# Late modulation products in a streaming encoder step: from the projection units into the rounds of the recurrence

## The reference

```python
def layer(x, c, attn_fn, wkv0, shift0, w_ada, b_ada, g_norm, w_in, ...):
    mod = jax.nn.silu(c) @ w_ada + b_ada                  # (1024) @ (1024, 6144), for two c
    sh1, sc1, gt1, sh2, sc2, gt2 = jnp.split(mod[:, None, :], 6, axis=-1)
    h = rmsnorm(x, g_norm[0]) * (1 + sc1) + sh1
    z = h @ w_in                                          # 5376 columns
    ...                                                   # band attention; token shift
    o_b, wkv1 = rwkv7_time_mix(zx, wkv0, ...)             # delta-rule recurrence, 8 heads
    merged = gates[..., :D_MODEL] * (o_a @ w_out_attn) + gates[..., D_MODEL:] * (o_b @ w_out_rwkv)
    x = x + gt1 * (merged @ w_out)
    h2 = rmsnorm(x, g_norm[1]) * (1 + sc2) + sh2
    u, gg = jnp.split(h2 @ w_ffn_in, 2, axis=-1)
    x = x + gt2 * ((jax.nn.silu(gg) * u) @ w_ffn_out)
```

## Time and profile before

| | |
|---|---|
| median of three runs | 1021.21 us (1020.38 to 1023.74) |
| the profiled execution | 1022.72 us, its span in the trace 1021.0 us |
| busy share of the span | PE 96%, PEld 88%, DVE 66%, ACT 49%, POOL 34% |
| projection by seven products | 68 to 194 us of the span |
| rounds of the recurrence | 312.7 to 496 us, with the tail to about 520 us |
| granted PE clock | 0.996 of full |

### The profile page before, as it was taken

The page is one execution under the profiler, slowest core; times in us unless marked ns, Lnnn a source line. Parts: engine busy times, 40 slices in busy tenths (PEclk is TensorE's granted clock), DMA queues, the critical chain, the costliest instruction groups (busy, mean ns, idle before and its releaser), DMA issues.

```text
span 1021.0 us, 26935 instructions
## 1 busy us (share of the span) xinstructions
PE 978.5 (96%) x10820; PEld 893.8 (88%) x10820; DVE 670.6 (66%) x1420; ACT 496.3 (49%) x1118; POOL 344.7 (34%) x341
## 2 busy tenths in 40 slices
PE   6999999999999999898899999999999999999996
PEld 4898888999997677666798999999999999999996
DVE  4985565595036666666547566888888887966724
ACT  4565655463444454545242255555555555723423
POOL 1156432153313260600260455343343343043340
PEclk9999999999999999999999999999999999999998
DMA  9967676483301000020342632223323323222312
GB/s 355 393 180 258 208 250 232 157 273 117 119 35 50 14 13 24 13 87 4 129 124 73 215 102 82 83 82 100 106 82 97 109 82 98 87 83 78 115 37 88
DMA packets 107372, 123.50 MB, mean 121 GB/s; under 512 B 5300, under 2 KB 91488, under 8 KB 104840
## 3 DMA queue, kind: packets, MB, share of 16 engines
q1 hardware_dynamic: 102048, 112.97, 34.0%
q10 hardware_dynamic: 5224, 9.10, 2.8%
HBM read 109.45 MB, written 15.23 MB: 122 GB/s over the span
## 4 chain that ended last, share of the span: by engine, by line
PE 85%; DVE 7%; ACT 4%; issue 2%; POOL 1%; ACTq 1%; DVEq 0%
PE ps L2460 45%; PE ps L3132 22%; PE ps L2658 11%; PE ps L3198 4%; PE ps L2873 1%; DVE s_sb L1925 1%; PE ps L2773 1%; DVE hl L1616 1%; DVE Pb L1896 1%; ACT x_sq L977 0%; POOL w_lo L765 0%; DVE XX L1906 0%; PE ps L3217 0%; POOL w_lo L930 0%; ACTq L963 0%
## 5 line engine op out<-in xcount | busy, mean ns | idle before, releaser
L924 POOL TENSOR_TENSOR ws_lo<-w_raw,ws_hi 128x512 fp32r<-128x512 f32 x63 | 80.5, 1292 | 146.2 <-DVE ps L2179 132.5
L765 POOL TENSOR_TENSOR w_lo<-w_raw,w_hi 128x2048 fp32r<-128x2048 f32 x11 | 50.7, 4608 | 140.6 <-ACT w_hi L987 123.8
L3132 PE MATMUL ps<-th,ws_hi 128*128 128x274 f32 x336 | 97.6, 291 | 0.0
L3132 PE MATMUL ps<-tl,ws_hi 128*128 128x274 f32 x336 | 97.6, 290 | 0.0
L3132 PE MATMUL ps<-th,ws_lo 128*128 128x274 f32 x336 | 97.2, 289 | 0.0
L2460 PE MATMUL ps<-hh,w_hi 128*128 128x274 f32 x448 | 95.7, 298 | 1.4 <-DVE hl L1616 0.7
L2460 PE MATMUL ps<-hl,w_hi 128*128 128x274 f32 x448 | 92.9, 291 | 2.4 <-DVE al L2261 2.1
L2460 PE MATMUL ps<-hh,w_lo 128*128 128x274 f32 x448 | 93.4, 292 | 0.0
L2460 PEld LDWEIGHTS ps<-hh,w_hi 128*128 128x128 f32 x448 | 71.7, 191 | 7.2 <-issue 5.8
L2186 DVE TENSOR_TENSOR ws_lo<-ps,ws_hi 128x512 fp32r<-128x512 f32 x84 | 57.3, 684 | 28.8 <-ACT ws_hi L1384 28.8
L3132 PE MATMUL ps<-hh,ws_hi 128*128 128x274 f32 x252 | 74.8, 297 | 0.6 <-ACT rest L1409 0.3
(11 more groups left out here) (549 smaller groups left out, 3031.4 us busy)
## 6 DMA issues: line engine op xcount, KB each, us to landing
w_raw<-in_w_ffn_in SPq DMA_DIRECT2D x44, 512.0 KB, 4.9
w_raw<-in_w_in SPq DMA_DIRECT2D x42, 512.0 KB, 5.8
ada_l<-in_w_ada SPq DMA_DIRECT2D x16, 1024.0 KB, 5.0
ada_w<-in_w_ada SPq DMA_DIRECT2D x8, 1024.0 KB, 13.4
w_raw<-in_w_ffn_out SPq DMA_DIRECT2D x16, 512.0 KB, 3.5
g_d<-gst SPq DMA_DIRECT2D x16, 274.0 KB, 2.6
gring<-g_d SPq DMA_DIRECT2D x16, 274.0 KB, 3.7
w_raw<-in_w_out SPq DMA_DIRECT2D x8, 512.0 KB, 4.6
```

What stands on the lines that cost most here:

```text
L765: pool.tensor_tensor(w_lo[:, s, 0:cols], w_raw[:, s, 0:cols], w_hi[:, s, 0:cols].bitcast(F32), ALU.subtract).then_inc(lo_done, 1)
L924: pool.tensor_tensor(slot_of(ws_lo, p), block_source(s, p), slot_of(ws_hi, p).bitcast(F32), ALU.subtract) .then_inc(wslo_done, 1)
L3132: ins = pe.matmul(product_out(s, p), wt[:, w], xt[c], start=fresh and c == 0 and j == 0, stop=c == HK - 1 and j == 2, skip_group_check=not ...
```

## The change

- The 16 late blocks leave `proj_seven`, with their two copies, flips and bias adds.
- They come back as 32 pieces. Piece m belongs to row block k = m // 4 and column quarter b = m % 4, and takes both sections: two sections by four strips of 32 partitions, 128 columns each, 8 matmuls in the code, 16 in the trace. Sections share the bank by a shift of the stationary window (`c_columns`), so that section 1 lands in rows 0 and 1 and section 2 in rows 2 and 3 of each strip.
- Pieces run in phases 4, 7, 8 and 10 of every round, behind the level products of the phase and ahead of its `p_attn`. A piece uses bank 3, which the recurrence leaves free in these phases.
- A row block is complete after one round. DVE adds the bank to a sum in SBUF (`late_add`, at phase 10, ahead of that phase's attention work on DVE); PE waits for it at phase 12. One flip (`late_flip`) and the bias adds go into the tail's first two levels.
- SP issues the loads of piece m when piece m - 2 is done: for even m two transfers of 256 KB, for odd m four (two of 192 KB and two of 64 KB). All rows are 512 bytes. The first two are issued ahead of the first K and V slices, and the first half of w_out_attn moves behind the loads of piece 29.

```diff
+        LATE_P = [16 * r + p for r in range(NR_) for p in (4, 7, 8, 10)]
...
+            def late(m):
+                (k, b), q = late_at(m), m % 2
+                if m >= 2:
+                    sp.wait_ge(late_used, m - 1)
+                for i in range(2):
+                    w = ada_rows(1 + i, k).rearrange("p (j b c) -> p j b c", j=4, c=P)[:, :, b, :]
+                    if q == 0:
+                        sp.dma_start(late_w[i][:, :, :], w).then_inc(late_in[0], 16)
+                    else:
+                        sp.dma_start(late_w[2 + i][:, :, :], w[:, 0:3]).then_inc(late_in[1], 16)
+                        sp.dma_start(late_last[i][:, :], w[:, 3]).then_inc(late_in[1], 16)
...
             for hp in range(HP):
+                asked = late_until(32 * hp - 15, asked)
                 if hp:
                     sp.wait_ge(kct_mm, hp)
                 sp.dma_start(kc_raw[:, :, :], ...)
+                asked = late_until(32 * hp - 2, asked)
...
+            def late_add(k):          # DVE
+                got, out = ps[:, LATE_BANK, :], late_sum[:, :, :].rearrange("p b c -> p (b c)")
+                dve.wait_ge(late_used, 4 * k + 4)
+                if k:
+                    dve.wait_ge(late_added, ADDED + k)
+                    tt(out, got, out, ALU.add).then_inc(late_added, 1)
+                else:
+                    dve.wait_ge(rg_out, RG_OUT + 16 * HP)
+                    dve.tensor_copy(out, got).then_inc(late_added, 1)
...
+                if p == 10:
+                    late_add(rnd)
                 v_attn(g)
...
+            def late_piece(m):        # PE
+                (k, b), q = late_at(m), m % 2
+                pe.wait_ge(late_in[q], 16 + (32, 64)[q] * (m // 2 + 1))
+                if b == 0 and k:
+                    pe.wait_ge(late_added, ADDED + k)
+                for i in range(2):
+                    for j in range(4):
+                        w = late_w[2 * q + i][:, j, :] if q == 0 or j < 3 else late_last[i][:, :]
+                        ins = pe.matmul(ps[32 * j:32 * j + 32, LATE_BANK, b * P:(b + 1) * P], c_columns(k, 1 + i), w,
+                                        start=i == 0, stop=i == 1)
+                ins.then_inc(late_used, 1)
...
-                    g = 7 * (i - U_PS) + p
-                    if g % 4 == 3 and g // 4 < NLATE:
-                        late(g // 4)
...
+                for m, u in enumerate(LATE_P):
+                    if u == g:
+                        late_piece(m)
                 if g:
                     p_attn(g)
```

More of the change, by code:

```diff
@@ L99, in build @@
         par = at("par", [P, N1 + N2], PERS + 1536)
[L100 to L103, removed]
+        sc2 = at("sc2", [P, KD * 32 + 8], PERS + 2080)
+        mod = at("mod", [P, 6 * KD, 2], PERS + 3136)
+        gsc = at("gsc", [P, 2, KD, 2], PERS + 3520)
+        stat = at("stat", [P, 16], PERS + 3648)
         shc = stat[:, 0:4].rearrange("p (n s) -> p n s", n=2)
[L105 to L107 removed]
+        omka = at("omka", [P, HP], PERS + 3520)
+        shst = at("shst", [P, 2, ZT], E + 76512)
+        ind = at("ind", [P, HP, 32], E + 73792)
         shrow = at("shrow", [2 * ZT, P], PERS + 512)
@@ L138, in build @@
         ada_w = [at(f"ada_w{k}", [P, UC], a) for k, a in enumerate(ADDR_EARLY)]
-        ada_l = [at(f"ada_l{q}", [P, UC], a) for q, a in enumerate(ADDR_LATE)]
+        late_w = [at("late_w0", [P, 4, P], HI + 4608), at("late_w1", [P, 4, P], RAW),
+                  at("late_w2", [P, 3, P], HI + 6656), at("late_w3", [P, 3, P], RAW + 6656)]
+        late_last = [at("late_l2", [P, P], RAW + 2048), at("late_l3", [P, P], PERS + 512)]
+        late_sum = at("late_sum", [P, 4, P], E + 74304)
         HK, QB = KD // 2, KD // 2 * P
@@ L407, in nth, with c_columns, late_at @@
             return base + per * (i - U_PS) + n
-        NLATE = (NSEC - 1) * KD
-        NFLIP = NSEC + 1
+        NLATE, NEARLY = KD * 4, 2
+        LATE_BANK, FLIP_BANK = 3, 5
+        def c_columns(k, sec):
+            return sc2[:, 32 * k + (0, 2, 0)[sec]:32 * k + (0, 2, 0)[sec] + 32]
+        def late_at(m):
+            return m // 4, m % 4
         T_QKV = 1
@@ L646, in _, with late_until @@
             sp.wait_ge(lo_done, U_OA)
+            late_free = [LATE_P[m - 2] for m in range(2, NLATE)]
+            def late_until(u, m):
+                while m < NLATE and late_free[m - 2] <= u:
+                    late(m)
+                    m += 1
+                return m
+            sp.wait_ge(shift_out, 32)
+            sp.wait_ge(unit_mm, U_OA)
+            sp.wait_ge(rg_out, RG_OUT + 16 * HP)
+            for m in range(2):
+                late(m)
+            asked = 2
             for hp in range(HP):
+                asked = late_until(32 * hp - 15, asked)
                 if hp:
@@ L1572, in _ @@
             p1 = lambda c: par[:, c:c + 1]
-            link(dve.memset(sc2[:, :, :], 0.0))
+            link(dve.memset(sc2[:, :], 0.0))
             dve.memset(ssq[TS:2 * TS, TT:KS], float(D))
@@ L2036, in _ @@
                     attn_part(0)
+                if lev == 1:
+                    dve.wait_ge(ada_tr, NEARLY + 1)
+                    mod_added(1)
+                    mod_added(2).then_inc(mod_set, 1)
+                    dve.wait_ge(mod_set, NEARLY + 1)
+                    scales(1)
             chain(7)
@@ L2499, in rstd_spread, with late_flip @@
                 ins.then_inc(xd_mm, 1)
[L2501 to L2510, removed]
+            def late_piece(m):
[9 more added lines that the diff above has]
+                ins.then_inc(late_used, 1)
+            def late_flip():
+                pe.wait_ge(late_added, ADDED + KD)
                 for b in range(4):
-                    ins = pe.transpose(ps[:, ACC, b * P:(b + 1) * P], ada_sb[:, b * P:(b + 1) * P], ident[:, :])
+                    ins = pe.transpose(ps[:, FLIP_BANK, b * P:(b + 1) * P], late_sum[:, b, :], ident[:, :])
                 ins.then_inc(ada_tr, 1)
@@ L2989, in _ @@
                 p_level_x(NT, lev)
+                if lev == 0:
+                    late_flip()
                 if lev < 3:
```

60 lines of the change are left out of this document (16 added, 44 removed).

## The result

The changed kernel takes 1027.62 us (median of 5 runs, 1025.16 to 1028.32), the kernel before 1021.21: ratio 1.0053, 95% interval 1.0035 to 1.0071. It is slower by 6.4 us, where I forecast 0.9 faster, and it lies outside my range. The profiled execution has a span of 1026.6 us against 1021.0, so 5.6 more.

A forecast was written before the change was run, and what follows sets the result against it. PE was taken as the bound, busy all 124.00 us of the projection and 188.40 of 208.00 in the recurrence. Terms -19.8 + 13.1 + 5.2 + 0.6 = -0.9 gave 1020.3 us from 1021.21, range 1017.5 to 1023.5.

The forecast's parts named there:

- What goes, -19.8: Projection: removing sixteen late blocks and two flips takes 19.8 us off PE's path.
- The rival in which the projection gives nothing back: Projection: block products newly wait for their weights, 0.5 us a unit, +5, so 1025; chance 0.09.
- A piece, 0.57: Recurrence: each piece costs PE 0.45 us plus 0.12 for one more change of form.
- the rival of weight loads in series: Pieces: weight loads not loaded ahead stand in series with matmuls, 32 x 0.43 = +13.8, so 1034; chance 0.14.
- The rounds, 4 x (1.40 + 1.88) = 13.1: Recurrence: pieces add 1.40 us to each even round and 1.88 to each odd one, over four pairs.
- the term of 0.68 for `late_add`: Odd rounds, phase 10: DVE works without pause, so the inserted add lengthens the round by 0.68 us; even rounds hide it.
- The stand for the fourth piece, 1.3 in each even round: Even rounds, phase 10: PE waits 1.3 us for piece 3's loads, issued only after piece 1; 5.2 us in four rounds.
- In the other places there is time: Recurrence: all loads other than the even rounds' fourth piece land before PE needs them, so no wait is counted.
- I count no change of it: Both stretches: granted clock stays 1.00, the 2.4 GHz level, as PE is never idle for long; no cost.
- The tail, 0.6: Tail: one flip costs PE 4 x 0.11 + 0.12 = 0.6 us; the bias adds cost nothing.
- The rival of the long stand: Even rounds' fourth piece: loads take 4.1 us to land, +5.6, so 1026; chance 0.06.
- The rival of loads in time: Even rounds' fourth piece: loads arrive in time and the 5.2 us go, -6.1, so 1015.1; chance 0.20.

The follow-up runs named there:

- Experiment 4: The changed kernel with the late blocks removed and brought back nowhere (no loads, pieces, adds or flip): 1000.21 us, ratio 0.9789 to the kernel before.
- experiment 9: Pieces at phases 4, 5, 8, 10 and gates later, as experiment 7, with `late_add` cut from 512 columns to 4 after the first round: 1014.46 us, ratio 0.9926.
- Experiment 5: The kernel of experiment 3, with PE made to wait behind seven pieces for GpSimd clearing a small tile, no transfer in it: 1037.13 us, ratio 1.0131.
- experiment 3: The changed kernel with only the first two pieces' data loaded and used by all 32 pieces: 1013.82 us, ratio 0.9916 to the kernel before.
- experiment 7: The changed kernel with pieces at phases 4, 5, 8, 10 and the three gates' transfers queued behind the last late loads: 1015.70 us, ratio 0.9944.
- 10: The kernel of experiment 7 again, on the same chip as experiment 9: 1014.96 us, ratio 0.9939 to the kernel before.
- experiment 8: The kernel of experiment 7 with even rounds at phases 4, 6, 8, 10 and odd ones at 4, 5, 8, 10: 1015.96 us, ratio 0.9938.
- experiments 1: The changed kernel with each round's second piece in phase 5 instead of 7, nothing else edited: 1017.59 us, ratio 0.9957 to the kernel before.
- 11: The changed kernel with pieces at phases 4, 5, 8, 10 alone, run again on a third chip: 1016.03 us, ratio 0.9951 to the kernel before.

## Why the prediction was wrong, by its steps

- **What goes, -19.8:** right. 19.7 by the start of the recurrence. Experiment 4, with nothing brought back, is 20.5 us shorter than before by the spans and 21.6 by the medians. In its profile the recurrence starts 19.3 us earlier, so 1.2 us lie behind that point; 0.8 of them come between 660 and 860 us, as told above, without a cause that I know. The rival in which the projection gives nothing back is out.
- **A piece, 0.57:** right to the hundredth, and with it the rival of weight loads in series is out (it needed 0.12 more, and the rounds without loads come out at 11.15 and not near 13.1 + 13.8).
- **The rounds, 4 x (1.40 + 1.88) = 13.1:** the even rounds are right (1.21 to 1.44). The odd ones are right in rounds 3 and 5 (1.80, 1.87) and 0.8 too dear in rounds 1 and 7 (1.06, 1.04). The sum is 11.15 by the profile. Its reason in phase 10 fell: the term of 0.68 for `late_add` on VectorE is worth at most 0.5 us in one round (experiment 9), so what fills the 1.8 in rounds 3 and 5 is something else, and I have not settled what, nor in which phase.
- **The stand for the fourth piece, 1.3 in each even round:** the place and the cause are right, the size is not. Measured 1.93, 1.30, 2.24, 1.89, in all 7.4 for 5.2. PE came 2.7 us after the load was asked for, close to the 2.65 worked out (my last issue at 373.87 should have been 372.58 + 1.26 = 373.84; nothing hangs on that), but 3.4 in round 4, where it had stood 0.56 for the piece before. In rounds 0 and 6 the last of the four issues came 2.3 and 2.2 us after the first instead of 1.26, because one issue took 1.35 and 1.26 us instead of 0.49; in round 4 the landing took 4.1 us instead of 2.7. In the other three the last slice, of 64 KB, landed sooner than my 2.7, in 2.3 to 2.6 us; so the 1.30 of round 2 agrees with my 1.3 by two errors that cancel (1.4 us of issues and 2.6 of landing for 1.26 and 2.7). Timeline of SP of the changed kernel, round 0:

```profile
305.85 0.37 SPq L602 DMA_DIRECT2D late_w<-in_w_ada  x1
306.26 1.35 SPq L603 DMA_DIRECT2D late_l<-in_w_ada  x1
307.65 0.44 SPq L602 DMA_DIRECT2D late_w<-in_w_ada  x1
308.13 0.49 SPq L603 DMA_DIRECT2D late_l<-in_w_ada  x1
```

- **"In the other places there is time":** mostly, not wholly. Pieces of two transfers stood 0.28, 0.56 and 1.05 us, 1.9 together. I had taken a landing of 2.7 for a slice of 256 KB; these landed in 2.7 to 5.2, with a median of 3.5 (page of the changed kernel, part 6: issues, KB, us to landing):

```profile
late_w<-in_w_ada SPq DMA_DIRECT2D x32, 256.0 KB, 3.5
```

- **"I count no change of it" (the clock):** this is the step that failed, and the dearest: 7.2 us. I had shown that PE is never idle for long in the kernel *before* and carried that over to a kernel into which I myself had put stands. Experiment 5 shows that stands of this length bring the low clock with no late load near, experiment 3 that without the loads the clock is not low in the rounds.
- **The tail, 0.6:** nothing was added there by the profile (7.9 us behind at the end of the rounds, 7.7 at the first residual).
- **Sum:** the terms that I had come to -19.7 + 11.15 + 7.4 = -1.2, close to my -0.9. The 1.9 of stands elsewhere and the 7.2 of clock make it +7.9; the 2.1 that come back behind the recurrence and 0.1 in the tail bring the profile to 5.6. The rival of the long stand named 1026 by a landing of 4.1 us in every even round; it hit the time better than its cause, since only one landing was that long. The rival of loads in time, 1015.1, is what experiments 7 and 10 measured once the loads were nearly all in time (1015.7, 1015.0), though with the second piece at another place and the gates later; it was the better sum for a kernel that I had not built.

## What to carry to other kernels

Price a stand of PE by more than its length: here each stand of 1.7 us or more in the recurrence also brought a stretch at the lower clock, worth 1.6 to 2.9 us in the change and some 3 in experiment 5. A load that waits for the piece two places back has only the time between those two pieces; place the pieces by the loads' time (here 3.8 to 5.7 us from the first of four issues to the last landing), not only by PE's gaps. A place two phases earlier was worth 10 us, with no instruction more or less.

## What the runs showed of the hardware that I had not expected

- In the recurrence the clock went low behind each of the five stands of 1.68 to 2.63 us of experiment 5, and not behind 0.72 and 1.20 there, or 1.30 in the change. The line is not sharp: the stand of 2.12 us in the feed-forward part, the same in every kernel, has a low stretch behind it in seven of the thirteen profiles and none in six, the change and experiment 7 among them; in experiment 8 a wait of 1.33 us in round 7 has one and in 7 the same wait does not. The Trainium skill ("TensorE: Matmul & The Clock Gate", Part 1) says that the gate follows how busy PE has been; experiment 5 agrees, as the DMA share in the first windows behind its stands is 0.00 to 0.02.
- The low stretch lasts 3.4 to 6.8 us in the change and 10 to 14 in experiment 5. Why it differs stays open.
- PE can stand for 1.2 to 1.9 us with nothing to wait for, at a fixed place in its program, when three transfers of 274 KB run there (experiments 1 and 11 against 7 and 10). It starts again 1.4 us behind the end of a 16 KB packet of the instruction queue. That packet starts 1.8 and 1.7 us after the 8 KB instruction packet before it in 1 and 11, and 0.0 to 0.3 us after it in 7, 9 and 10. That the transfers hold it up I infer; no row times it from its request.
- An issue on SP that takes 0.49 us as a rule took 1.26 to 1.35 in two of the four stands. What it waited for no view shows.
